# Second layer of a three-layer block on one core: the product of probabilities and values as three f32r products of high and low halves

## The reference, cut to what matters

```python
def mla_layer(x, pos, ...):            # 16 heads, A_V = 128
    z = rms_norm_2(x, norm_g) @ w_in
    ...
    q = rms_norm_2(q, q_gain); k = rms_norm_2(k, k_gain)
    ...
    o = mla_attend(q, k, v, pos)       # softmax(q k^T + causal mask) v
    return x + (o * jax.nn.silu(gate)) @ w_out
```

## Time and profile before

| | us |
|---|---|
| median of 3 runs (3125.1 to 3125.4) | 3125.38 |
| the profiled execution's own time | 3124.12 |
| its span in the trace | 3122.3 |
| TensorE busy in the span | 3085.4 (99%) |
| VectorE busy | 1768.3 (57%) |
| ScalarE busy | 1274.4 (41%) |
| GpSimd busy | 215.4 (7%) |

### The profile page before, as it was taken

The page is one execution under the profiler, slowest core; times in us unless marked ns, Lnnn a source line. Parts: engine busy times, 40 slices in busy tenths (PEclk is TensorE's granted clock), DMA queues, the critical chain, the costliest instruction groups (busy, mean ns, idle before and its releaser), DMA issues. The chain is left out here.

```text
span 3122.3 us, 51762 instructions
## 1 busy us (share of the span) xinstructions
PE 3085.4 (99%) x21393; PEld 2539.7 (81%) x21393; DVE 1768.3 (57%) x3073; ACT 1274.4 (41%) x2328; POOL 215.4 (7%) x170
## 2 busy tenths in 40 slices
PE   8999999999999999999999999999999999999999
PEld 6877777777778778788888888888888888888787
DVE  5335565656666754644457776335556656665822
ACT  4124343434434422524346665323344434443521
POOL 0000000001011101000111121110000000000000
PEclk9999999999999999999999999999999999999999
DMA  8433333342232353343331213534223323332452
GB/s 252 126 81 92 91 88 98 100 115 61 67 98 71 108 176 108 112 106 104 107 102 55 61 55 119 162 108 118 88 81 95 95 75 101 95 95 82 161 164 79
DMA packets 494639, 324.25 MB, mean 104 GB/s; under 512 B 27194, under 2 KB 449693, under 8 KB 494406
## 3 DMA queue, kind: packets, MB, share of 16 engines
q1 hardware_dynamic: 494374, 320.94, 35.1%
q10 hardware_dynamic: 32, 0.01, 0.0%
HBM read 276.05 MB, written 44.85 MB: 103 GB/s over the span
## 5 line engine op out<-in xcount | busy, mean ns | idle before, releaser
L550 DVE TENSOR_TENSOR WLT<-AR,WHT 128x1024 fp32r<-128x1024 f32 (+1 forms) x430 | 527.2, 1232 | 655.7 <-ACT WHT L544 654.9
L562 PE MATMUL PS<-XH,WHT 128*128 128x512 f32 (+1 forms) x2224 | 888.3, 399 | 2.7 <-DVE AR L1045 1.4
L564 PE MATMUL PS<-XH,WLT 128*128 128x512 f32 (+1 forms) x2224 | 867.5, 390 | 0.0
L544 ACT ACTIVATE WHT<-AR 128x1024 fp32r<-128x1024 f32 (+1 forms) x430 | 447.5, 1043 | 597.5 <-PE PS L564 464.1
L563 PE MATMUL PS<-XL,WHT 128*128 128x512 f32 (+1 forms) x1712 | 666.9, 390 | 0.0
L562 PEld LDWEIGHTS PS<-XH,WHT 128*128 128x128 f32 (+1 forms) x2224 | 416.3, 187 | 99.1 <-issue 9.3
L564 PEld LDWEIGHTS PS<-XH,WLT 128*128 128x128 f32 (+1 forms) x2224 | 416.0, 187 | 91.0
L563 PE MATMUL PS<-ARR,WHT 128*128 128x512 f32 x1024 | 398.6, 389 | 0.0
L563 PEld LDWEIGHTS PS<-XL,WHT 128*128 128x128 f32 (+1 forms) x1712 | 320.5, 187 | 66.0 <-issue 2.4
L563 PEld LDWEIGHTS PS<-ARR,WHT 128*128 128x128 f32 x1024 | 192.4, 188 | 39.4 <-issue 0.2
L562 PE MATMUL PS<-XL,WHT 128*128 128x512 f32 x512 | 199.7, 390 | 0.4 <-issue 0.4
(11 more groups left out here) (512 smaller groups left out, 5152.6 us busy)
## 6 DMA issues: line engine op xcount, KB each, us to landing
AR<-b_w_in SPq DMA_DIRECT2D x128, 512.0 KB, 4.0
AR<-w_in SPq DMA_DIRECT2D x122, 512.0 KB, 3.9
AR<-a_w_in SPq DMA_DIRECT2D x48, 512.0 KB, 4.6
AR<-w_out SPq DMA_DIRECT2D x32, 512.0 KB, 4.2
AR<-a_w_out SPq DMA_DIRECT2D x32, 512.0 KB, 3.9
AR<-b_w_out SPq DMA_DIRECT2D x32, 512.0 KB, 4.0
proj_scratch<-AR SPq DMA_DIRECT2D x33, 256.0 KB, 2.1
residual_scratch<-RES SPq DMA_DIRECT2D x8, 1024.0 KB, 6.1
```

What stands on the lines that cost most here:

```text
L544: self.nc.scalar.activation(self.shaped(self.high, n), self.shaped(self.raw, n), ACT.Copy).then_inc(self.s_high, 1)
L550: self.nc.vector.tensor_tensor(self.shaped(self.low, n), self.shaped(self.raw, n), f32(self.shaped(self.high, n)), ALU.subtract).then_inc( ...
L562: mm(out, wh, xh[k0 + c], start=(start and c == 0), stop=False)
L564: last = mm(out, wl, xh[k0 + c], start=False, stop=(stop and c == nk - 1))
```

## The change

The probabilities and the values are split too. ScalarE's two copies write f32r high halves (`PTR`, `VTR`) in place of the f32 tiles. VectorE gets two new functions that read the same PSUM banks after ScalarE and subtract the high half: `turned_low(i,u)` (two instructions of 128x512, one for each head) and `value_low(i,j)` (one of 128x512). `values` issues three f32r matmuls for each one before. Waits for a free bank are moved from ScalarE's copy to VectorE's subtraction. The places of the new calls in VectorE's order are in the diff.

```diff
@@ -195,6 +195,7 @@
         self.AR = self.sb("AR", [P, ARENA])
         self.ARR = nc.alloc_sbuf_tensor_at("ARR", [P, KT, T], F32R, offset=at + 4 * 8 * T)
         self.SQR = nc.alloc_sbuf_tensor_at("SQR", [P, 2, T], F32R, offset=at + 4 * 24 * T)
+        self.RSR = nc.alloc_sbuf_tensor_at("RSR", [P, T], F32R, offset=at + 4 * 31 * T)
         at = aligned(nc)
         self.EXT = self.sb("EXT", [P, EXTRA, T])
         self.EXTR = nc.alloc_sbuf_tensor_at("EXTR", [P, EXTRA, T], F32R, offset=at)
@@ -2525,6 +2526,10 @@
     PT = XB[:, 0:4, :].rearrange("p a t -> p (a t)").rearrange("p (e b q) -> p e b q", e=2, b=TB)
     VT = XB[:, 4:6, :].rearrange("p a t -> p (a t)").rearrange("p (b n) -> p b n", b=TB)
     HI = XB[:, 6:8, :]
+    PTR = k.XL[:, 0:4, :].rearrange("p a t -> p (a t)").rearrange("p (e b q) -> p e b q", e=2, b=TB)
+    VTR = k.XL[:, 4:6, :].rearrange("p a t -> p (a t)").rearrange("p (b n) -> p b n", b=TB)
+    PTL = [x.rearrange("p a t -> p (a t)").rearrange("p (b q) -> p b q", b=TB) for x in (k.ARR[:, 9:11, :], k.STGR)]
+    VTL = [x.rearrange("p (b n) -> p b n", b=2) for x in (k.ARR[:, 11, :], k.RSR)]
     KPR, RSA = (k.AR[:, n * T:(n + 1) * T] for n in (30, 31))
     RM, RS, RQ, KS = take(24, 1), take(16, 1), [take(8, 1), take(8, 1)], take(8, 1)
     MX, GK, KPC = take(12, 1), take(1, 1), take(TB, 1)
@@ -2554,9 +2559,9 @@
               pool=["kl0", "kl1", "krl", "sa0", "sa1"],
               dve=["ck0", "ck1", "meank", "reck", "dg0", "dg1", "kg0", "kr0", "kg1", "kr1", "qg", "cqh0", "cq0", "cqh1", "cq1", "meanq", "recq", "rq"])
     W = Marks(k, "mlar", dve=["sws", "qc", "qa"], act=["sw", "qrh"], pool=["qrl"])
-    V_ = Marks(k, "mlav", pe=["a", "b"], act=["a", "b"])
+    V_ = Marks(k, "mlav", pe=["a", "b"], act=["a", "b"], dve=["a", "b"])
     S = Marks(k, "mlas", pe=[f"s{u}" for u in steps], dve=[f"{x}{u}{e}" for u in steps for e in heads for x in "bm"], act=[f"x{u}{e}" for u in steps for e in heads])
-    R = Marks(k, "mlat", dve=[f"{x}{u}{e}" for u in steps for e in heads for x in "rp"], pe=[f"t{u}{e}" for u in steps for e in heads], act=[f"c{u}{e}" for u in steps for e in heads])
+    R = Marks(k, "mlat", dve=[f"{x}{u}{e}" for u, xs in ((0, "rp"), (1, "rp"), (0, "l"), (2, "rp"), (1, "l"), (2, "l"), (3, "rp"), (3, "l")) for e in heads for x in xs], pe=[f"t{u}{e}" for u in steps for e in heads], act=[f"c{u}{e}" for u in steps for e in heads])
     for i in range(NP):
         st.by[KU[i]] = lambda eng, i=i: N.wait(eng, i, "pe.k1")
         st.by[QRU[i]] = lambda eng, i=i: N.wait(eng, i, "pe.qr")
@@ -2713,7 +2718,7 @@
             def key_factors(i, e):
                 N.wait(pe, i, f"dve.dg{e}")
                 if i:
-                    V_.wait(pe, i - 1, f"act.{'ab'[e]}")
+                    V_.wait(pe, i - 1, f"dve.{'ab'[e]}")
                 for tb in steps:
                     last = nc.tensor.transpose(FB[e][:, blk(tb)], SQ[:, e, blk(tb)], ident)
                 N.did(last, "pe", f"rk{e}")
@@ -2764,9 +2769,9 @@
                 for e in heads:
                     R.wait(pe, i, f"dve.p{u}{e}")
                     if u:
-                        R.wait(pe, i, f"act.c{u - 1}{e}")
+                        R.wait(pe, i, f"dve.l{u - 1}{e}")
                     elif i:
-                        R.wait(pe, i - 1, f"act.c3{e}")
+                        R.wait(pe, i - 1, f"dve.l3{e}")
                     else:
                         pe.wait_ge(a_evac, AT)
                     for b in range(TB):
@@ -2774,15 +2779,18 @@
                     R.did(last, "pe", f"t{u}{e}")
 
             def values(i, j):
-                R.wait(pe, i, f"act.c{2 * j + 1}1")
-                V_.wait(pe, i, "act.b")
+                R.wait(pe, i, f"dve.l{2 * j + 1}1")
+                V_.wait(pe, i, "dve.b")
                 if j:
                     O.wait(pe, i, "dve.o0")
                 else:
                     O.wait(pe, i - 1, "dve.o1")
                 for e in heads:
                     for b in range(TB):
-                        last = mm(OB[:, half(e)], VT[:, b, blk(e)], PT[:, e, b, :], start=(b == 0), stop=(b == TB - 1))
+                        vh, vl, ph, pl = VTR[:, b, blk(e)], VTL[b // 2][:, b % 2, blk(e)], PTR[:, e, b, :], PTL[e][:, b, :]
+                        mm(OB[:, half(e)], vh, ph, start=(b == 0), stop=False)
+                        mm(OB[:, half(e)], vh, pl, start=False, stop=False)
+                        last = mm(OB[:, half(e)], vl, ph, start=False, stop=(b == TB - 1))
                 O.did(last, "pe", f"v{j}")
 
             def out_unit(n, h, part=None):
@@ -2791,7 +2799,7 @@
                         N.wait(pe, NP - 1, "dve.meanq")
                         O.wait(pe, 3, "dve.lo")
                     else:
-                        V_.wait(pe, NP - 1, f"act.{'ab'[n - 1]}")
+                        V_.wait(pe, NP - 1, f"dve.{'ab'[n - 1]}")
                 elif h == 1:
                     pe.wait_ge(o_evac, n - 2)
                 elif n == 0 and part == 0:
@@ -2971,7 +2979,7 @@
             def value_copy(i, j):
                 V_.wait(act, i, "pe." + "ab"[j])
                 O.wait(act, i - 1, "pe.v1")
-                V_.did(A(VT[:, 2 * j:2 * j + 2, :], FB[j][:, :].rearrange("p (b n) -> p b n", b=2), ACT.Copy), "act", "ab"[j])
+                V_.did(A(VTR[:, 2 * j:2 * j + 2, :], FB[j][:, :].rearrange("p (b n) -> p b n", b=2), ACT.Copy), "act", "ab"[j])
 
             def exps(i, u):
                 for e in heads:
@@ -2987,7 +2995,7 @@
                     O.wait(act, i, "pe.v0")
                 for e in heads:
                     R.wait(act, i, f"pe.t{u}{e}")
-                    R.did(A(PT[:, e, :, blk(u % 2)], TBK[e][:, :].rearrange("p (b t) -> p b t", t=P), ACT.Copy), "act", f"c{u}{e}")
+                    R.did(A(PTR[:, e, :, blk(u % 2)], TBK[e][:, :].rearrange("p (b t) -> p b t", t=P), ACT.Copy), "act", f"c{u}{e}")
 
             def high(i):
                 O.wait(act, i, "dve.o1")
@@ -3249,6 +3257,24 @@
                     R.wait(dve, i, f"dve.r{u}{e}")
                     R.did(TS(x, x, MX[:, 8 + j:9 + j], None, ALU.mult), "dve", f"p{u}{e}")
 
+            def turned_low(i, u):
+                if i == 0 and u == 0:
+                    for j in halves:
+                        dve.wait_ge(ev_out[j], 16 * NP)
+                if u == 0:
+                    O.wait(dve, i - 1, "pe.v1")
+                if u == 2:
+                    O.wait(dve, i, "pe.v0")
+                for e in heads:
+                    R.wait(dve, i, f"act.c{u}{e}")
+                    x = PTL[e][:, :, blk(u % 2)]
+                    R.did(TTn(x, TBK[e][:, :].rearrange("p (b t) -> p b t", t=P), f32(PTR[:, e, :, blk(u % 2)]), ALU.subtract), "dve", f"l{u}{e}")
+
+            def value_low(i, j):
+                V_.wait(dve, i, "act." + "ab"[j])
+                O.wait(dve, i - 1, "pe.v1")
+                V_.did(TTn(VTL[j], FB[j][:, :].rearrange("p (b n) -> p b n", b=2), f32(VTR[:, 2 * j:2 * j + 2, :]), ALU.subtract), "dve", "ab"[j])
+
             def output(i, j):
                 O.wait(dve, i, f"pe.v{j}")
                 if j == 0:
@@ -3406,18 +3432,24 @@
                 scale(i, 1)
                 if not more:
                     st.split_low(dve, UT + 4 * i + 4)
+                turned_low(i, 0)
                 bias(i, 2)
                 if more:
                     key_means(q)
                     scale(i, 2)
+                    value_low(i, 0)
+                    turned_low(i, 1)
                     key_diagonals(q)
+                    value_low(i, 1)
                     keys(q)
                     bias(i, 3)
                     output(i, 0)
                     rotary_gain(q)
+                    turned_low(i, 2)
                     scale(i, 3)
                     st.split_low(dve, UT + 4 * i + 5)
                     query_copy(q, 0)
+                    turned_low(i, 3)
                     rotary_turn(q)
                     st.split_low(dve, UT + 4 * i + 6)
                     query_copy(q, 1)
```

## The result

| | before | after |
|---|---|---|
| median, us | 3125.38 (3125.1 to 3125.51) | 3206.29 (3204.78 to 3209.92) |
| profiled execution's own time, us | 3124.12 | 3204.78 |
| its span, us | 3122.3 | 3203.0 |

The ratio is 1.0262 [1.0248, 1.0276]: 80.9 us slower. The forecast was 3174 with a range to 3195, so the sign was right and the size was not: 49 us were foreseen.

A forecast was written before the change was run, and what follows sets the result against it. TensorE, busy 99% of the span, was taken as the bound. Stalls less savings add 5.85 us a step, 41 over steps 0 to 6, plus 4.4 (step 7) and 3.4 (clock): 49, so 3174, range 3158 to 3195.

The forecast's parts named there:

- Factor transposes: In each step TensorE waits 2.26 us for the late key diagonals, then 0.50 for `value_low(i,1)`.
- `turned(i,3)`: In each step TensorE stalls 0.4 us here, as `scale(i,3)` stands behind `turned_low(i,2)` in VectorE's queue.
- first sums: First `query_sums` of a step: TensorE waits 1.1 us for GpSimd's addition.
- second sums: Second `query_sums` of a step: TensorE waits 2.93 us for GpSimd's addition, behind the delayed square.
- The price of an addition: Each of ten new VectorE subtractions a step takes 0.62 us, bounds 0.55 and 0.68; 6.2 us a step.
- The saving of a call: A `values` call takes 2.88 us as f32r against 3.45, giving back 0.57 a call, 1.14 a step.
- the rival "hidden": VectorE's idle time hides the additions and only TensorE's saving of 9.1 us is left: 3116.3; chance 0.03.
- The port: `rotary_turn`'s last addition takes 0.69 us, not 1.66, as GpSimd is idle then; otherwise 0.96 more a step.
- Step 7: Stalls of 1.6 us at `turned(7,1)` and 3.9 at the second output unit; with 1.14 back, +4.4 us.
- The clock: One fall of TensorE's clock to half rate beside a stall, +3.4 us; bounds 0 and eight falls, 27.
- the 53 that the prediction named as its sign of being wrong: A loop step of about 49.8 us was forecast; under 45 or over 53 would make the prediction wrong.
- The rival: The clock falls at nearly every long stall: eight times 3.4 us, 3198; chance 0.08.

The follow-up runs named there:

- experiment 4: The changed kernel with `values` as one f32 product again, the ten subtractions and their waits kept; 3189.54 us, 1.02.
- experiment 5: The changed kernel without the subtractions: f32r products take the high halves three times, TensorE waits for ScalarE's copies; 3123.83 us, 0.9991.
- the reordered kernel, experiment 6: The changed kernel with VectorE's queue reordered in both halves of a step and in step 7; 3129.02 us, 1.0005.
- experiment 3: The changed kernel with filler matmuls at all three waits: factor transposes, first sums and second sums; 3177.82 us, 1.0164.
- Experiment 1: The changed kernel with ten filler matmuls before the factor transposes and twelve before the second sums; 3185.33 us, 1.0187.
- experiment 7: The changed kernel with VectorE's queue reordered only in the second half of a step; 3158.65 us, 1.01.
- experiment 2: The changed kernel with twelve filler matmuls before the second sums alone; 3185.46 us, 1.0188.
- experiment 8: The changed kernel with VectorE's queue reordered only in the first half of a step; 3177.75 us, 1.0164.
- experiment 11: The second mended order (3128.23 us) with the rotary sum behind the second query copy, and ScalarE's square and GpSimd's addition earlier; 3139.28 us, 1.0044.
- experiment 10: A further VectorE order of the changed kernel: `low` and `turned_low(i,1)` earlier, `turned_low(i,3)` back behind `rotary_turn`; 3128.23 us, 1.0005.

## Why the prediction was right in sign and too small

- **The waits**: right, place by place. Factor transposes 2.26 and 0.50, measured 2.24 and 0.16 to 0.4; `turned(i,3)` 0.4, measured 0.33; first sums 1.1, measured 1.09; second sums 2.93, measured 2.77. The profile counts a wait only from the end of the record before it. From start to start the second sums come 2.93 us late (3.05 us after the last matmul of `values`, in place of 0.12), the first 1.25, and the projections behind `turned(i,3)` 0.7. Following the timeline with each engine's queue gave the delays to some 0.3 us.
- **The price of an addition**: 0.62 from start to start, measured 0.60 to 0.61. ScalarE's copies with an f32r output cost nothing more: 0.58 to 0.61.
- **The saving of a call**: 0.57 forecast for 2.88 us; measured 2.95 to the next function, in a call at full rate, and a gain of 0.50 (experiment 4). The second call's is swallowed by the wait behind it (experiments 4 and 5). The forecast had that in its 2.93, since it let TensorE arrive there earlier, so its sum was not wrong by this; the rival "hidden", with 9.1 us of pure gain, was.
- **The port**: 0.69 instead of 1.66, as forecast, since GpSimd is idle there; in the reordered kernel it is 1.66 beside GpSimd again.
- **Step 7**: waits of 1.6 and 3.9 forecast, 1.50 and 3.67 measured.
- **The clock**: the step that failed. "I put one such fall into the sum, +3.4; bounds 0 and eight of them, 27." The trace shows 14 stretches at half rate in the loop, behind the second sums in seven steps, at the factors in six and once in step 7, worth 28.5 us at least (experiment 3) and 36 at most. They also carry the step to 54.6 us, past the 53 that the prediction named as its sign of being wrong. The rival had one a step at 3198, and got 0.08; even it had only one place of the two and 3.4 us for each, and stayed 8 below the measurement. The argument against it was that the clock's one fall before came out of a thin stretch, and that a dense `values` call shields the wait. The call doesn't shield it: in the change `values(i,1)` ends just before each of the seven second waits, and the clock falls at all seven. Experiment 1 has it fall even after 1.1 us of wait and 0.9 of one-column sums, with projections before them and `values` behind. The Trainium skill (TensorE: Matmul & The Clock Gate, HAM oscillation — how this bites in real kernels) warns of just this, gaps in a loop that bring the clock down each time round; the trace agrees, with 6.8 us at half rate in each of seven steps and 3.4 more in six.
- **The rest**: with the clock kept up in steps 0 to 6 the change costs 51 us where 45 were forecast, at most 1.7 of them for the stretch left in step 7. A step is 0.65 us longer (50.45 for 49.8). Most of that can be read off: `turned(i,3)` costs 0.7 and not 0.4, the first sums 1.25 and not 1.1, and two calls give back 1.0 and not 1.14.

The range ended at 3195 because it allowed three falls more. With the clock at both places in each step (half of 6.8 + 3.4, 5.1 us a step, 36 in seven) the same sum would have given 3171 + 36 = 3207. That it meets the 3206 so closely is partly luck: step 0 had no fall at its factors and step 7 had one that nobody forecast, and the waits cost up to 6 us more than their part of the sum.

## What to carry to other kernels

When an instruction is added to an in-order queue, ask what stands behind it and whether its own input is there: here 6.2 us of subtractions in an engine with 10 us to spare cost 81 us in one order and 2 in another (in which some older instructions moved too). On a TensorE that is busy throughout, a new wait of 1 to 3 us each time round a loop has a second price, the clock behind it (here 28 to 36 us on 52 us of waits); put it into the upper bound for every wait and every round. How many rounds pay it was not to be foreseen here: the same wait of 2.23 us at the factors brought a fall in six of seven steps in the change and in three of seven in experiment 7. And a saving ahead of a wait is no saving.

## What was not expected of the hardware

- The granted clock in the records is still full through most of a wait and falls about where TensorE is back at work: 1.00 until 1754.3, and half from there on, 0.3 us before the sums start.
- Small pauses can suffice, but the same pause doesn't always. 1.1 us and the one-column sums behind it were followed by a fall in four of seven steps in experiment 1, in three in experiment 4, in one in experiments 2 and 8, and in none in the change. The 2.23 us at the factors were followed by one in six steps in the change, in five, four and three in experiments 2, 4 and 7. Waits of 0.40, 0.78 and 0.85 in one step brought one in each (experiment 11), waits of 0.3 or 0.4, 0.7 and 0.5 in none (experiments 6 and 10). What decides it was not found.
- The faster product in place of the slower one made the changed kernel slower, by 17 us: the wait behind it was 2.77 us long and not 2.19, and the stretches at half rate were 6.8 us where they were 3.4.
